# One change to a two-layer hybrid encoder kernel: expert slots stored once, scaling moved to ScalarE, parameters loaded in two parts, additions ahead of a weight block

## The reference

```
proj   = norm(x) @ w_in          -> qa, fa, ia, ga | qb, kb, vb | gate_a, gate_b
ya     = HGRN2 recurrence (4 heads of 128 x 128, chunks of 64)
yb     = windowed attention (8 query heads, 2 key heads of 64; q and k normed, times q_norm, k_norm, q also times 64 ** -0.5)
x     += (sigmoid(gate_a) * (ya @ w_pa) + sigmoid(gate_b) * (yb @ w_pb)) @ w_o
x     += layer 0: swiglu(norm(x))           (width 3584)
         layer 1: sum over the top 2 of 8 experts of gate * swiglu_e(norm(x))
x     += sigmoid(norm(x) @ w_ple_gate) * (p @ w_ple_up)
```

## Time and profile before

| | us |
|---|---|
| median of 3 runs | 1644.59 |
| lowest and highest run | 1643.84, 1645.05 |
| the profiled execution's own time | 1644.34 |
| its span, first to last instruction | 1642.2 |

### The profile page before, as it was taken

How to read it: one execution, slowest core, us unless ns; L and a number is a source line. 1 busy time by engine, 2 the same in 40 slices (tenths; PEclk the granted TensorE clock), 3 DMA queues, 4 the chain that set the end, 5 groups by cost and what they waited for, 6 DMA issues and landing times.

```text
span 1642.2 us, 22205 instructions
## 1 busy us (share of the span) xinstructions
PE 1621.3 (99%) x8525; PEld 1332.1 (81%) x8525; DVE 1290.3 (79%) x1082; ACT 1093.5 (67%) x907; POOL 80.3 (5%) x71
## 2 busy tenths in 40 slices
PE   8999999999999999999999999999999999999998
PEld 6878888888888787888888888888888888888886
DVE  7776654454578777988888998988988888888886
ACT  6565544444555656778778778778778778778774
POOL 0100000000001000100000000000000000000100
PEclk9999999999999999999999999999999999999999
DMA  9444555555454345999999999999999999999991
GB/s 334 163 155 154 179 187 185 192 185 199 166 190 139 131 167 212 382 393 351 392 393 344 395 395 347 391 391 346 393 395 339 396 393 354 390 389 349 393 400 47
DMA packets 202002, 480.15 MB, mean 292 GB/s; under 512 B 8928, under 2 KB 11552, under 8 KB 201952
## 3 DMA queue, kind: packets, MB, share of 16 engines
q1 hardware_dynamic: 198128, 466.16, 77.6%
q0 software_dynamic: 3680, 13.24, 2.9%
q10 hardware_dynamic: 144, 0.04, 0.0%
HBM read 470.89 MB, written 8.39 MB: 292 GB/s over the span
## 4 chain that ended last, share of the span: by engine, by line
PE 91%; DVE 6%; issue 2%; ACT 1%; DMA 0%; ACTq 0%; DVEq 0%
PE ps L1493 28%; PE ps L1495 28%; PE ps L1494 28%; PE ps L1909 2%; DVE w_lo L903 2%; PE ps L1505 1%; PE ps L1502 1%; PE ps L1500 1%; PE ps L1501 1%; PE ps L1508 1%; ACT w_hi L573 0%; DVE arena L1017 0%; DVE arena L993 0%; PE ps L1941 0%; PE ps L1791 0%
## 5 line engine op out<-in xcount | busy, mean ns | idle before, releaser
L903 DVE TENSOR_TENSOR w_lo<-raw,w_hi 128x2048 fp32r<-128x2048 f32 x440 | 1002.3, 2290 | 219.7 <-ACT w_hi L573 218.1
L573 ACT ACTIVATE w_hi<-raw 128x2048 fp32r<-128x2048 f32 x440 | 842.9, 1918 | 331.9 <-PE ps L1495 326.5
L1493 PE MATMUL ps<-w_hi,hT_hi 128*128 128x512 f32 (+1 forms) x1544 | 609.0, 394 | 3.9 <-DVE w_lo L903 1.8
L1495 PE MATMUL ps<-w_hi,hT_lo 128*128 128x512 f32 (+1 forms) x1544 | 599.3, 388 | 0.0
L1494 PE MATMUL ps<-w_lo,hT_hi 128*128 128x512 f32 (+1 forms) x1544 | 598.8, 388 | 0.0
L1493 PEld LDWEIGHTS ps<-w_hi,hT_hi 128*128 128x128 f32 x1544 | 290.6, 188 | 68.8 <-DVE w_lo L903 7.1
L1495 PEld LDWEIGHTS ps<-w_hi,hT_lo 128*128 128x128 f32 x1544 | 290.3, 188 | 60.9
L1494 PEld LDWEIGHTS ps<-w_lo,hT_hi 128*128 128x128 f32 x1544 | 290.8, 188 | 55.8
L1493 PE MATMUL ps<-w_hi,inner_hi 128*128 128x512 f32 x592 | 233.7, 395 | 0.0
L1495 PE MATMUL ps<-w_hi,inner_lo 128*128 128x512 f32 x592 | 230.8, 390 | 0.0
L1494 PE MATMUL ps<-w_lo,inner_hi 128*128 128x512 f32 x592 | 230.5, 389 | 0.0
(11 more groups left out here) (262 smaller groups left out, 824.0 us busy)
## 6 DMA issues: line engine op xcount, KB each, us to landing
raw<-in_w_moe_gate SPq DMA_DIRECT2D x112, 1024.0 KB, 8.0
raw<-in_w_moe_up SPq DMA_DIRECT2D x112, 1024.0 KB, 7.9
raw<-in_w_moe_down SPq DMA_DIRECT2D x112, 1024.0 KB, 8.2
raw<-in_w_in SPq DMA_DIRECT2D x37, 1024.0 KB, 5.7
raw<-in_w_dense_gate SPq DMA_DIRECT2D x14, 1024.0 KB, 5.1
raw<-in_w_dense_up SPq DMA_DIRECT2D x14, 1024.0 KB, 5.1
raw<-in_w_dense_down SPq DMA_DIRECT2D x14, 1024.0 KB, 5.0
raw<-in_w_o SPq DMA_DIRECT2D x8, 1024.0 KB, 5.0
```

The costliest lines, as they stand in the source:

```text
L573: nc.scalar.activation(w_hi[:, n % SLOTS, :], raw[:, n % RAW_SLOTS, :], ACT.Copy).then_inc(high_ready, 1)
L903: nc.vector.tensor_tensor(w_lo[:, n % SLOTS, :], raw[:, n % RAW_SLOTS, :], w_hi[:, n % SLOTS, :].bitcast(F32), ALU.subtract).then_inc(low_ ...
L1493: nc.tensor.matmul(o, x_parts[0][x_cols], parts[0], start=first, stop=False)
L1495: return nc.tensor.matmul(o, x_parts[1][x_cols], parts[0], start=False, stop=last)
```

## The change

- **Slots.** Each token writes two entries (token, gate) with four indirect DMAs from POOL into slot_rows in HBM, at a row that VectorE computes (`place_codes`); the rows were filled with padding from POOL in layer 0. One load brings all items' slots back. slot_table remains only for item 0; make_picks and take_slots in the items go; each item reads its slots in step 4 and makes its spread masks in step 5.
- **Bookkeeping.** over_experts, place_codes, place_gates and extras run in steps 0 to 3 of item 0, which VectorE now has ahead of its loop. VectorE splits the first expert block ahead of the gates.
- **Queries and keys** are scaled by ScalarE, with q_scale made once.
- **Parameters** in two parts: g_mix first, the rest (now in 6 loads) flipped within the first weight block.
- **Last additions** ahead of a weight block: the last keep_up of an item goes, and one stands behind the additions.

```diff
@@ gpsimd, fetch_slots (behind the stores of x_sum and x_rows)
                 nc.gpsimd.memset(pool_spare[:, :], 0.0).then_inc(spare_written, 1)
+                pool.wait_ge(codes_ready, 1)
+                pool.wait_ge(entries_ready, 1)
+                pool.wait_ge(slot_rows_stored, 16)
+                for t in range(TILES):
+                    for n in range(TOP_K):
+                        pool.wait_ge(spare_written, TOP_K * t + n + 1)
+                        nc.gpsimd.tensor_tensor(pool_spare[:, :], minus_half[:, 0:1], minus_half[:, 0:1],
+                                                ALU.add).then_inc(spare_written, 1)
+                        nc.gpsimd.indirect_dma_start(out=slot_rows[:, :], out_offset=bass.IndirectOffsetOnAxis(codes[:, t, n:n + 1], 0),
+                                                     in_=entries[:, t, n, :], in_offset=None).then_inc(slot_rows_stored, 16)
+                pool.wait_ge(slot_rows_stored, 16 + 16 * TILES * TOP_K)
+                pool.wait_ge(spare_written, TILES * TOP_K + 1)
+                nc.gpsimd.tensor_tensor(pool_spare[:, :], minus_half[:, 0:1], minus_half[:, 0:1], ALU.add).then_inc(spare_written, 1)
+                pool.dma_start(slots[:, :, :], slot_rows[:, :].rearrange("(s i) c -> s i c", i=ITEMS)).then_inc(slot_rows_loaded, 16)
+                spares = TILES * TOP_K + 2
                 pool.wait_ge(routed, 1)
                 count = pool.value_load(n_items_i[0:1, 0:1], min_val=EXPERTS, max_val=EXPERTS + EXTRA)
...
@@ scalar, mixer
                 take(I, lambda t: i_tok[:, t, :], ACT.Copy)
+                act_e.wait_ge(q_scaled, 1)
+                act_e.wait_ge(qk_transposed, layer + 1)
+                nc.scalar.activation(kbT, banks(0)[:, 0:SEQ], ACT.Copy,
+                                     scale=params[:, K_GAIN + layer:K_GAIN + layer + 1]).then_inc(qkT_ready, 1)
                 level_exp(4)
+                for n, bank in enumerate((UP, TRB)):
+                    last = nc.scalar.activation(qbT[:, 2 * n:2 * n + 2, :], banks(bank).rearrange("p (h t) -> p h t", h=2), ACT.Copy,
+                                                scale=q_scale[:, layer:layer + 1])
+                last.then_inc(qkT_ready, 1)
                 level_exp(5)
...
@@ vector, mixer
-                level_step(layer, 3, scale_keys)
-                nc.vector.tensor_scalar(qbT.rearrange("p (b h) t -> p b (h t)", b=2), ps[:, UP:TRB + 1:2, :],
-                                        params[:, Q_GAIN + layer:Q_GAIN + layer + 1], HEAD_DIM ** -0.5,
-                                        ALU.mult, ALU.mult).then_inc(qkT_ready, 1)
+                level_step(layer, 3)
...
@@ vector, route
-                extra_places()
-                dve.wait_ge(counted, 1)
-                count = dve.value_load(n_items_i[0:1, 0:1], min_val=EXPERTS, max_val=EXPERTS + EXTRA)
-
+                keep_up(UP1 - 1)
                 dve.wait_ge(route_exps, TILES)
...
-                extra_gates()
...
+            def place_codes():
...
+                link(nc.vector.scalar_tensor_tensor(code_base, column[:, 0:EXPERTS].unsqueeze(1).to_broadcast(tokens), 1.0 - ITEMS,
+                                                    chosen[:, :, :], ALU.add, ALU.mult))
+                nc.vector.scalar_tensor_tensor(code, place[:, :, :], float(ITEMS), code_base, ALU.mult, ALU.add)
...
+            def place_gates():
+
+                link(nc.vector.tensor_tensor(first_gate, gate_w[:, :, :], first_code, ALU.mult))
+                nc.vector.reduce_sum(entries[:, :, 0, 1], first_gate, AX_X)
+                link(nc.vector.tensor_tensor(first_code, gate_w[:, :, :], first_gate, ALU.subtract))
+                nc.vector.reduce_sum(entries[:, :, 1, 1], first_code, AX_X).then_inc(entries_ready, 1)
...
@@ vector, experts
-                        if s == 0:
-                            make_picks(bass.ds(t + 1, 1))
-                        if s == 2:
-                            dve.wait_ge(slots_done, t + 2)
+                        if first and s == 0:
+                            over_experts()
+                        if first and s == 1:
+                            place_codes()
+                        if first and s == 2:
+                            place_gates()
+                        if first and s == 3:
+                            extras()
+                        if s == 4:
+                            dve.wait_ge(slot_rows_loaded, 16)
                             dve.wait_ge(sums_stored, t * 16 + 48)
                             nc.vector.tensor_copy(sum_token[:, :], slot_token[:, :]).then_inc(sum_token_ready, 1)
...
-                    keep_up(MOE + PER_ITEM - 1, t)
                     dve.wait_ge(slot_copied, t + 1)
+                item(0, True)
+                split[0] -= PER_ITEM
+                dve.wait_ge(counted, 1)
+                count = dve.value_load(n_items_i[0:1, 0:1], min_val=EXPERTS, max_val=EXPERTS + EXTRA)
+                with dve.Fori(1, count) as t:
+                    item(t)
                 dve.wait_ge(x_summed, 16)
...
@@ vector, embedding
                 if layer:
+                    keep_up(base - 1, items, end)
                     norm_low(5, PLE_GAIN + KD, range(4, KD))
...
@@ tensor, experts
                         if s == 1:
                             pe.wait_ge(item_y_ready, t * 2 + 2)
-                            pe.wait_ge(picks_ready, t + 2)
                             pe.wait_ge(ple_up_taken, TILES)
-                            slot_table(slice(0, 1 + ITEMS))
...
@@ tensor, start
-            pe.wait_ge(params_loaded, 16 * PARAM_DMAS)
-            nc.tensor.transpose(banks(TRB)[:, 0:PARAM_ROWS], param_rows[0:PARAM_ROWS, :],
-                                ident[0:PARAM_ROWS, 0:PARAM_ROWS]).then_inc(params_transposed, 1)
+            pe.wait_ge(gains_first, 16)
+            nc.tensor.transpose(banks(TRB)[:, 0:MIX_ROWS], param_rows[0:MIX_ROWS, :],
+                                ident[0:MIX_ROWS, 0:MIX_ROWS]).then_inc(params_transposed, 1)
```

More of the change, by code:

```diff
@@ L264, in build_trunk @@
         extra_of = sb("extra_of", [P, EXTRA, EXPERTS])
-        item_place = sb("item_place", [P, TILES, ITEMS])
-        slot_columns = sb("slot_columns", [P, TILES, 1 + ITEMS])
-        item_gate_w = slot_columns[:, :, 0:ITEMS]
+        slot_columns = sb("slot_columns", [P, TILES, 2])
+        slots = sb("slots", [P, ITEMS, 2])
+        entries = sb("entries", [P, TILES, TOP_K, 2])
+        codes = sb("codes", [P, TILES, TOP_K], I32)
+        code_max = sb("code_max", [P, TILES])
+        code_sum = sb("code_sum", [P, TILES])
+        code_base, code_over, code, first_code, first_gate = (pair_b[:, :, n, :] for n in range(5))
         slot_now = sb("slot_now", [P, 3])
@@ L550, in _ @@
                 heads_rstd(2 * layer + 1, TILES * HEADS)
+                if layer == 0:
+                    pool.wait_ge(pads_written, 1)
+                    pool.dma_start(slot_rows[:, :].rearrange("(s i) c -> s i c", i=ITEMS), slots[:, :, :]).then_inc(slot_rows_stored, 16)
                 if layer:
@@ L1269, in route @@
                 link(nc.vector.scalar_tensor_tensor(place[:, :, :], place_ps, 1.0, chosen[:, :, :], ALU.add, ALU.mult))
-                link(nc.vector.tensor_scalar(item_place[:, :, 0:EXPERTS], place[:, :, :], -1.0, None, ALU.add))
-                make_picks(slice(0, 1))
+                for t in range(TILES):
+                    last = nc.vector.tensor_scalar(pick[:, t, :], column[:, :], 1.0, place[:, t, 0:1], ALU.add, ALU.is_equal)
+                last.then_inc(picks_ready, 1)
                 link(nc.vector.reduce_max(top[:, :], logits[:, :, :], AX_X))
@@ L1330, in make_picks @@
-            def make_picks(item):
-                for t in range(TILES):
-                    last = nc.vector.tensor_scalar(pick[:, t, :], column[:, :], item_place[:, t, item], None, ALU.is_equal)
-                last.then_inc(picks_ready, 1)
-            def take_slots(dst, item):
-                table = banks(TRB)
-                nc.vector.tensor_copy(dst[:, 0:1], table[:, item])
-                nc.vector.tensor_scalar(dst[:, 1:2], table[:, ITEMS:ITEMS + 1], float(SEQ), None, ALU.add)
-                return nc.vector.tensor_scalar(dst[:, 2:3], table[:, ITEMS:ITEMS + 1], float(SEQ - P), None, ALU.add)
+                link(nc.vector.reduce_sum(extra_expert[:, :], extra_of[:, :, :], AX_X))
@@ L1582, in column_unit @@
                         flip_x(norm, 1)
+                    if norm == 0 and k == 1:
+                        flip_other_params()
                     if norm is not None and k % 2 == 0:
@@ L1867, in gather_first, with slot_table @@
                         last.then_inc(gathered, 1)
-            def slot_table(columns_of):
+            def slot_table():
                 for n in range(TILES):
-                    for slots in CHUNKS:
-                        last = mm(banks(TRB)[slots, columns_of], pick[:, n, slots], slot_columns[:, n, columns_of],
```

(3 more changed lines are left out.)

150 lines of the change are left out of this document (85 added, 65 removed).

## The result

The changed kernel takes 1631.93 us (median of four runs, 1631.22 to 1632.20) against 1644.62 for the kernel before on the same chip: ratio 0.9923, 95% interval 0.9905 to 0.9940. The profiled execution took 1632.15 us around a span of 1630.4, 12.19 less than the 1644.34 of before.

A forecast was written before the change was run, and what follows sets the result against it. The prediction took TensorE, busy 99% of the span, as the bound; its terms, -1.1 - 0.6 - 1.6 + 0.85 - 4.2 - 0.8 = -7.45 us, took 1644.34 to 1636.9, range 1634.0 to 1642.0.

The forecast's parts named there:

- The mixers: Scaling off VectorE removes TensorE's wait at level product 5: net gain 0.3 us in each layer, 0.6 in sum.
- The start: First transpose of the parameters needs only g_mix: gain 1.1 us, between 0.75 and 1.45.
- the discount of 0.7: At the start, slow products end at the same moment as before, so 3.2 more run slowly, losing 0.7 us.
- Entry and item 0: Entry of the experts gains 1.6 us, item 0's bookkeeping loses 0.85, its dropped table pieces gain 0.53.
- the hole of the codes: Item 0, step 1 gets ten operations, 1.65 us on VectorE with 1.0 in hand: 0.65 lost.
- Items: TensorE drops eight table pieces of 64 x 13 in every item: 0.53 us each, 4.2 over eight.
- End: VectorE adds before it subtracts the second gate block, so TensorE's last flips come sooner: gain 0.8 us.
- The chain of stores: Item 0, step 4: VectorE's added wait for slots and first add takes 30.8 of 32.9 us, costing nothing.
- Rival (a): Stores in item 0 held up by VectorE's subtractions, two TensorE blocks each, late by 5.4 us: 1641.9; 15 in 100.
- (b): Items keep their length because the loads or VectorE set their pace: 1641.2 us; 8 in 100.
- (c): Stores and add in item 0 at their upper bounds, late by 13.1 us, kernel slower: 1649.5; 4 in 100.
- (d): No gain at the start and the experts' entry, without 1.1 and 1.6 us: 1639.6; 8 in 100.

The follow-up runs named there:

- table_in_items: The changed kernel with eight matmul pieces of 64 x 13 put back into step 1 of every item on TensorE alone; 1634.83 us.
- warm_and_split: The changed kernel with ten unread identity flips on TensorE before the flips of x, and half of place_codes moved to step 0 of item 0; 1631.61 us.
- keys_back: The changed kernel with the keys alone scaled on VectorE again; 1632.78 us.

## Why the prediction was wrong

**The mixers, the step that failed.** "TensorE waits 0.45 for it, and as long in layer 1: 0.5 each", net 0.3, with a bound of 1.0 in all. That VectorE comes 1.8 us sooner was right; that only the wait ahead of level product 5 hung on it was wrong. VectorE's exponents, ScalarE's exponential, w_hi, w_lo and VectorE's weights are one serial chain through levels 5 to 8, and TensorE met it four times in each layer: ahead of level product 5 (0.45 of the gain in mixer 0), within it (1.03 us in the earlier trace rows, 0.76 after; 0.29), at the flips of the probabilities (0.50) and at level product 8 (0.59). Each wait covers only what the waits before it have left, so together they are as long as the chain is late. 1.83 and 1.81 us were measured, 3.0 more than forecast in sum. The waits were on the list of waits, 2.2 and 0.9 us, and I had read the timeline at one place only. The delay of the gate projection by the keys, taken as 0.2, was 0.08 (offset 1.47 before it, 1.39 at it).

**The start.** 1.1 forecast, 1.47 in the profiles. The first product came 1.70 sooner (1.45 assumed). The half speed did not end at the same moment as before, as the discount of 0.7 had it; it ended 1.95 sooner (13.28 for 15.23). But this moment is not fixed at all, see below. The second flip, put at nothing, took 0.2 where it fell between products at half speed (the lead went from 1.70 to 1.49), and from the tenth product (1.72) to the flips of the keys another 0.25 of the lead went in small pieces, whose cause stays open. And the prediction took from the page that the clock stood at full during the slow products; that was the page's way of showing a stretch without a record, see below.

**Entry and item 0.** 1.28 forecast, 1.66 measured. Product by product, the lead over the kernel before grows by 0.79 at the first hole (0.79 forecast) and by 1.56 up to behind the second (1.26), loses 0.26 up to the first flip (0.45), grows by 0.60 at the pieces of the table (0.53), loses 0.88 at the hole of the codes (0.65), and 0.15 in the rest (0.2 for the loop). The 0.60 of the table is no gain by itself here: with the pieces left in, the hole of the codes is 0.58 smaller (table_in_items).

**Items.** "0.53 each" was 0.61, over seven items 0.6 more than forecast. With the pieces alone put back the period is 119.71, 0.59 more: 0.54 stand at the pieces, as the prediction read from its row, and some 0.05 in the ten products behind them, which come 0.231 apart instead of 0.227. Why these are slower isn't shown.

**End.** -0.8 forecast, -0.76 measured, -0.72 when undone. Right.

**The chain of stores.** "It fits by 2.1 and costs nothing": in the profiled execution it cost nothing, but by luck, with 0.13 in hand. From the entries to the landing of the add it took 33.0 us where 30.8 were forecast; VectorE asked after 33.1 (32.9). Its parts were off both ways: the stores' issues took 2.92 and then 1.02, 0.99, 0.99 (3.54 and then 1.60 assumed), their landing 4.9 (3), the spare operations 1.48 to 2.11 (0.19 and then 1.16), the add's issue 3.56 (1.60). Rival (a) did not happen as it was put, with two blocks for each store, but its mechanism is there: it held the first store and the add, 1.9 and 2.0 us, and the row by which the prediction dismissed it was misread, see below.

**What remains** is 0.40 outside the span, forecast as unchanged. Of the rivals, (b), (c) and (d) did not happen. The range failed because the mixers' bound was set by the one wait that I had counted: 1.0 where 3.64 were measured. (Its good ends, with 0.2 for the bookkeeping, sum to 1634.5 and not 1634.2.)

## What to carry to other kernels

Before costing an edit to an engine that stands in a chain with others, add up TensorE's waits over the whole list that name any engine of this chain: moving work off the chain can pay back all of them, up to the work moved, and not only the nearest. An operation taken out of a stretch that already has a hole is worth less there than elsewhere. A long stall of TensorE can cost more than its length: those of 1.95 us and more here had products at half speed behind them. And a chain of DMAs that fits in one profile may not fit in the next: the landing of one add varied by about 1 us from kernel to kernel here, with 0.13 in hand.

## What the runs showed of the hardware

**Half speed after a stall, and at the start.** Behind waits of 1.95, 2.92 and 9.59 us products were 0.43 apart for eight to ten products, the granted clock 0.50; behind those of 0.59 to 1.11 in the kernel before and the changed one, and of 1.49 in warm_and_split, they kept 0.23. At the start the first product at full speed stood anywhere from 9.1 to 15.8 us, and not because of the work ahead of it: the changed kernel and keys_back do the same up to their first products (9.57 and 9.63), yet one reached full speed at 13.28 and the other had it from its first product on. This alone is 8 x 0.2 = 1.6 us, and could be a good part of the spread between runs of one kernel; that isn't shown, since only one run of each was profiled. The page shows the clock as full during the slow products, but this is no measurement: the trace holds no record of the clock before 15.2 us in the kernel before, 13.2 in the changed one and 8.7 in keys_back, and the views print a stretch without a record as full. From its first record on, which says full, the products are 0.23 apart. The Trainium skill, page "TensorE: Matmul & The Clock Gate", section "Seeing it yourself", warns that the clock's trace events are not to be relied on. In these kernels the records and the spacing of the products agree.

**Issues of indirect DMAs wait for a running subtraction** (w_lo = raw - w_hi on VectorE, line 943). POOL of the changed kernel, and VectorE beside it:

```profile
688.96 2.92 POOL L545 DMA_INDIRECT slot_rows<-entries,codes  x1 [0.19 <-issue]
...
693.70 1.02 POOL L545 DMA_INDIRECT slot_rows<-entries,codes  x1 [0.16 <-issue]
...
699.10 0.99 POOL L545 DMA_INDIRECT slot_rows<-entries,codes  x1 [0.16 <-POOL pool_spare L543]
704.98 0.86 POOL L549 TENSOR_TENSOR pool_spare<-minus_half 128x1 f32<-128x1 f32 x1 [4.89 <-DMA slot_rows<-entries,codes]
...
708.20 3.56 POOL L561 DMA_INDIRECT x_sum<-arena,sum_token  x1 [0.15 <-issue]
```

```profile
686.44 4.48 DVE L943 TENSOR_TENSOR w_lo<-raw,w_hi 128x2048 fp32r<-128x2048 f32 x2
...
693.88 2.29 DVE L943 TENSOR_TENSOR w_lo<-raw,w_hi 128x2048 fp32r<-128x2048 f32 x1 [0.39 <-ACT w_hi L604]
...
703.51 6.73 DVE L943 TENSOR_TENSOR w_lo<-raw,w_hi 128x2048 fp32r<-128x2048 f32 x3
```

The issue at 688.96 begins within a subtraction that ends at 686.44 + 4.48 = 690.92 and is done 0.96 after it. Those at 693.70 and 699.10 begin 0.2 to 0.7 before a subtraction, with VectorE idle or in another operation, and take 1.02 and 0.99. The add at 708.20 begins within the last of three that end at 710.24 and is done 1.52 after, where other adds take 1.59. So an issue that finds a subtraction running ends only after it; one that comes first goes through. All 14 profiles agree. Of the indirect issues on POOL from the experts on, the 123 that begin with no subtraction running took 0.98 to 1.65 us. The 121 that begin within one ended 0.86 to 0.96 after it (stores and gathers) or 1.52 to 1.58 (adds). The kernel before had such a case, too: its first add, the 3.54 of the prediction, ended 1.58 after the last of three subtractions.

```profile
653.79 6.70 DVE L903 TENSOR_TENSOR w_lo<-raw,w_hi 128x2048 fp32r<-128x2048 f32 x3 [0.23 <-DVE slot_now L1341]
```

```profile
658.53 3.54 POOL L533 DMA_INDIRECT x_sum<-arena,sum_token  x1 [0.19 <-POOL pool_spare L531]
```

The Trainium skill, page "SBUF — State Buffer", section "SBUF: two separate sides", says that whichever engine starts first holds the shared port pair for its whole instruction. The rows agree as far as POOL waits for VectorE. The other direction they don't show: the subtraction at 693.88 starts within an issue and takes 2.29, as long as any. The prediction had taken a short issue (772.71) as speaking against this page, but that one had started in VectorE's pause, between the subtraction that ended at 772.50 and the next.
